# Side products dealt anew, two waits reordered and token copies split in a one-core diffusion step with DeltaNet heads and experts

## The chip, the cores and the metric

The kernel is one program on one core of a Trainium2 chip. The metric is the device time in microseconds of one execution. Smaller is better.

## What is computed

One step of a trunk with one layer, for 128 context tokens and 1024 latent tokens of width 1024. The parts the change touches are the DeltaNet mixer and the expert mixture:

```python
q = l2norm(q) * (DN_HEAD_DIM ** -0.5); k = l2norm(k)      # 8 heads of width 128
decay = exp(where(incl, g[..., :, None] - g[..., None, :], -inf))
lmat = where(strict, einsum('bhnck,bhnsk->bhncs', k_beta, k) * decay, 0.0)
a = lmat + eye                      # unit lower triangular, inverted per chunk
sol = triangular_solve(a, rhs)      # rhs from v and k
attn = einsum('bhnck,bhnsk->bhncs', q, k) * decay
# scan over the chunks, once forward and once backward:
v_new = u_c - w_c @ S;  o_c = q_c @ S + attn_c @ v_new;  S = S * d_c + k_c^T @ v_new
o = o_f + flip(o_b)
o = o * rsqrt(mean(o * o, -1) + EPS) * onorm_g * silu(gate)
...
# experts: each of 16 picks 128 latent and 16 context tokens
xs = h[idx]
ys = ((silu(xs @ w_gate) * (xs @ w_up)) @ w_down) * gates
```

## The kernel before

The instructions of each engine are written out by hand, and semaphores order them. PE is TensorE, DVE is VectorE, ACT is ScalarE, POOL is GpSimd, SP is SyncE with its DMA queue. "Head" is one pass of `body_pe`, `body_act`, `body_dve` and `body_pool`. Heads 0 to 6 are a loop on PE, ACT and DVE; head 7 is written out behind it.

**Side products.** A head needs little of TensorE at a time, with copies between its steps. So the input projection of the next head and of the merge gates is dealt into the gaps. A unit of it is eight matmuls into one bank (line 604), of 512 columns or, where its name ends in 0, of 128. `fill(place)` issues `FILLS[place]` of these matmuls, `evac(place)` on ACT copies out the units that end there (line 635), through `units_until`. A head has 18 units, the last head 21. `place` names run in the order of `PLACES`.

**A head on PE.** `fill("start")`; the sums of squares of k (`nk`) and q (`nq`), line 744; transposes of k and v (`kT`, `vT`, line 752); products k k and k q (line 762), the second of which waits until DVE has copied v out of its banks; transposes `LT` (line 771); two turns `Y2`; then six levels of an inverse by blocks. In a level, for two directions and three groups of three tiles: `Z` (line 788), a fill, `P` (line 788), a fill, and the turn `X` (line 779), which ACT copies out (line 935) before the next level's `Z` may write. ACT copies `Z` of direction 0, DVE that of direction 1 (line 1049); DVE takes `P` by a masked copy (line 1057). Behind the levels come `res`, `fix` and a scan over nine tiles with a fill of one matmul between its steps. `fill("end")` issues what is left of the side products, and then PE turns the normalised o (line 868).

**Norms and decays.** ACT squares q and k into `dm_flat[0]` and `dm_flat[1]`, and the inverse norms (`Ln`, `Exp`) come into the same places. DVE multiplies q and k by them (lines 1006 and 1007), and then writes the arguments of the decays of both directions over them: nine instructions each, line 1012. Then it copies v (line 1017). ACT takes `Exp` of the decays (line 916) and copies the products (line 921); POOL masks the decays; DVE multiplies them by k k (line 1023) for `LT`.

**End of a head.** POOL adds and squares o, DVE sums it (line 1109), ACT takes `Ln` and `Exp` (lines 975 and 977), DVE multiplies (line 1111), PE turns, DVE multiplies by the gate (lines 1118 to 1122) and marks the head's end. ACT's `evac("end")` stands ahead of its `Ln`. SP then stores the result with `store_b` (line 669), whose semaphore is `b_out`.

**Experts.** For expert e, PE makes the gate and up products in eight tiles (line 1968), turns the gathered tokens of expert e+1 (`turn_in`, lines 1942 and 1944) and makes eight down tiles (line 1982) with two banks in turn: tile 2 waits until ACT has copied tile 0 (lines 2014 and 2015). ACT's `evac_in`, 16 copies of the turned tokens (lines 1997 and 2001), stands ahead of the copy of tile 0:

```python
        if not last_e:
            evac_in(act, e + 1)
        for dt in range(KD):
            act.wait_ge(sem("dn_filled"), e * KD + dt + 1)
```

Of the kernel before, what the change touches and what calls it, by code (L numbers as in the profile page):

```python
# [19 lines left out]
P = 128  # L20
# [58 lines left out]
def build(nc, a, out_p, out_s, out_sf, out_sb, dbg=None, stop=99):  # L79
    ctx = ExitStack()  # L80
    with ctx:
        sems = {}

        def sem(name):
            if name not in sems:
                sems[name] = ctx.enter_context(nc.semaphore(name))
            return sems[name]
# [463 lines left out]
        ORDER_LAST = ("g1", "g0", "A0", "B0", "g2", "A1", "A2", "B1", "B2") + tuple(f"{x}{i}" for x in "CDEF" for i in range(3))  # L551

        FILLS = {"start": 3, "nk": 5, "nq": 12, "kk": 12, "LT": 16, "Y2f": 8, "Y2b": 8, "res": 2, "fix": 4}
        FILLS |= {f"Z{b}": 3 for b in LEVELS} | {f"P{b}": 3 for b in LEVELS}
        FILLS |= {f"scan{t}{x}": 1 for t in range(1, NT) for x in "abc"}
        PLACES = ["start", "nk", "nq", "kk", "LT", "Y2f", "Y2b"] + [f"{x}{b}" for b in LEVELS for x in "ZP"] + ["res", "fix"]
        PLACES += [f"scan{t}{x}" for t in range(1, NT) for x in "abc"] + ["end"]

        def units_until(order, place):

            if place == "end":
                return len(order)
            return sum(FILLS[p] for p in PLACES[:PLACES.index(place) + 1]) // KD

# [106 lines left out]
        def sync4(sp):  # L671
# [56 lines left out]
            sp.wait_ge(sem("b_out"), 16 * H)  # L728
            sp.dma_start(bT3[:, 0:H - 1, :], b_dram[0:(H - 1) * P, :].rearrange("(k p) t -> p k t", p=P)).then_inc(sem("b_in"), 16)

        def body_pe(pe, h, last_h=False):
            order = ORDER_LAST if last_h else ORDER
            side_work = projections(pe, h, order)

            def fill(place):
                for _ in range(FILLS.get(place, UNITS_MAX * KD)):
                    next(side_work, None)
# [3 lines left out]
            for d, name in ((1, "nk"), (0, "nq")):  # L741
                pe.wait_ge(sem("sq_ready"), 2 * h + 2 - d)
                for b, (at, n) in enumerate(SPAN):
                    nc.tensor.matmul(TRI[d][b][:, 0:n], ones, dm_flat[d][:, at:at + n], start=True, stop=True).then_inc(sem(f"filled{d}"), 1)  # L744
                fill(name)

            for d, name in ((0, "kT"), (1, "vT")):
# [49 lines left out]
            for lv, b in enumerate(LEVELS):  # L797
                for d in range(2):
                    products(d, f"Z{b}", [(nL[d], Ys[d])])
                fill(f"Z{b}")  # L800
                for d in range(2):
                    products(d, f"P{b}", [(Xs[d], Zs[d])])
                fill(f"P{b}")
                for d in range(2):
                    turn(d, f"X{b}", Ys)


            for d in range(2):
# [47 lines left out]
            for t in range(1, NT):  # L856
# [4 lines left out]
                fill(f"scan{t}b")  # L861
                advance(t)
                fill(f"scan{t}c")
            fill("end")
            pe.wait_ge(sem("o_normed"), h + 1)
            for g in range(3):
                for i in range(3):
# [6 lines left out]
        def body_act(act, h, last_h=False):  # L874
# [6 lines left out]
            def silu(j):  # L881
                act.wait_ge(sem("conv_done"), 3 * h + CONV_TURN.index(j))
                alone(act)
                for n, at in ((CTX, 0), (LAT, LAT0)):
                    last = nc.scalar.activation(qkvg[j][:, at:at + n], (k_next if j == 1 else qkvg[j])[:, at:at + n], ACT.Silu)
                if j == 2:
                    last.then_inc(sem("v_ready"), 1)
                else:
                    last.then_inc(sem("qk_silu"), 1)
                    act.wait_ge(sem("qk_silu"), 2 * h + 2 - j)  # L890
                    nc.scalar.activation(dm_flat[j][:, 0:CTX], qkvg[j][:, 0:CTX], ACT.Square)
                    nc.scalar.activation(dm_flat[j][:, CTX:T], qkvg[j][:, LAT0:LAT0 + LAT], ACT.Square).then_inc(sem("sq_ready"), 1)

            silu(1)
            silu(0)
# [6 lines left out]
            for d in (1, 0):  # L902
                for b, (at, n) in enumerate(SPAN):
                    filled(act, h, d, ("nq", "nk")[d], b)
                    nc.scalar.activation(dm_flat[d][:, at:at + n], TRI[d][b][:, 0:n], ACT.Ln, bias=eps_c).then_inc(sem(f"drained{d}_act"), 1)
                all_drained(act, h, d, ("nq", "nk")[d])
                nc.scalar.activation(dm_flat[d], dm_flat[d], ACT.Exp, scale=-0.5, bias=qscale_c if d == 0 else 0.0).then_inc(sem("rnorm"), 1)
                evac(("nq", "nk")[d])

            for g in range(3):  # L910
                filled(act, h, 0, "kT", g)
                nc.scalar.activation(flat(ktok, g), TRI[0][g][:, 0:384], ACT.Copy).then_inc(sem("drained0_act"), 1)

            for d in range(2):
                act.wait_ge(sem("gdiff"), 2 * h + d + 1)
                nc.scalar.activation(dm_flat[d], dm_flat[d], ACT.Exp).then_inc(sem("decay_exp"), 1)
            act.wait_ge(sem("b_out"), 16 * h + 16)
            for d in range(2):
                for g in range(3):
                    filled(act, h, d, ("kk", "kq")[d], g)  # L920
                    nc.scalar.activation(kq_flat[d][:, g * 384:(g + 1) * 384], TRI[d][g][:, 0:384], ACT.Copy).then_inc(sem(f"drained{d}_act"), 1)
# [19 lines left out]
            for b in LEVELS:  # L941
                copy(0, f"Z{b}", Zs)
                evac(f"Z{b}")
                evac(f"P{b}")
                for d in range(2):
                    copy(d, f"X{b}", Xs, F16)
            copy(0, "res", Zs)
            evac("res")
            evac("fix")
# [16 lines left out]
            for t in range(1, NT):  # L966
# [3 lines left out]
                evac(f"scan{t}b")  # L970
                outputs(t)
                evac(f"scan{t}c")
            evac("end")
            act.wait_ge(sem("o_sumsq"), h + 1)
            nc.scalar.activation(orow, orow, ACT.Ln, scale=1.0 / P, bias=eps_c).then_inc(sem("o_ln"), 1)
            act.wait_ge(sem("o_ln"), h + 1)
# [3 lines left out]
            for n, at in ((CTX, 0), (LAT, LAT0)):  # L980
                last = nc.scalar.activation(gateT[:, at:at + n], gateT[:, at:at + n], ACT.Silu)
            last.then_inc(sem("gate_ready"), 1)

        conv_to = (qT, k_next, vT)

# [15 lines left out]
            ins.then_inc(sem("tap_done" if tap < TAPS - 1 else "conv_done"), 1)  # L1001

        def body_dve(dve, h, last_h=False):
            for d, name in ((1, "k_normed"), (0, "q_normed")):
                dve.wait_ge(sem("rnorm"), 2 * h + 2 - d)
                nc.vector.tensor_tensor(qkvg[d][:, 0:CTX], qkvg[d][:, 0:CTX], dm_flat[d][:, 0:CTX], ALU.mult)
                nc.vector.tensor_tensor(qkvg[d][:, LAT0:LAT0 + LAT], qkvg[d][:, LAT0:LAT0 + LAT], dm_flat[d][:, CTX:T], ALU.mult).then_inc(sem(name), 1)
            for d in range(2):
                dve.wait_ge(sem(f"head_in{d}"), 32 * h + 32)
                dve.wait_ge(sem("q_normed" if d == 0 else "k_normed"), h + 1)  # L1010
                for t in range(NT):
                    last = nc.vector.tensor_scalar(dm_flat[d][:, t * P:(t + 1) * P], grow[d][:, t * P:(t + 1) * P],
                                                   tab["gc"][:, t, bass.ds(h + d * H, 1)], 0.0, ALU.subtract, ALU.min)
                last.then_inc(sem("gdiff"), 1)
            for g in range(3):
                filled(dve, h, 1, "vT", g)
                nc.vector.tensor_copy(flat(vtok, g), TRI[1][g][:, 0:384]).then_inc(sem("drained1_dve"), 1)

            for d in range(2):
                dve.wait_ge(sem("decay_masked"), 2 * h + d + 1)  # L1020
# [277 lines left out]
def later(nc, a, v, out_p, out_s, dbg, stop):  # L1298
# [691 lines left out]
        body9_pe(pe, E - 1, last_e=True)  # L1990
        turn_out(pe, E - 1)

    def evac_in(act, e):

        act.wait_ge(sem("xsT_filled"), e + 1)
        for k in range(KD):
            nc.scalar.activation(xsT[:, k, 0:CAP_L], banks[k // 4][:, (k % 4) * P:(k % 4 + 1) * P], ACT.Identity,  # L1997
                                 scale=amp2T[:, 1, k:k + 1], bias=modT3[:, 1, 3 * KD + k:3 * KD + k + 1])
        for k in range(KD):
            q, j = k // NJ, k % NJ  # L2000
            last = nc.scalar.activation(xsT[:, k, CAP_L:CAP], banks[2][:, j * QROWS + q * CAP_C:j * QROWS + (q + 1) * CAP_C], ACT.Identity,  # L2001
                                        scale=amp2T[:, 0, k:k + 1], bias=modT3[:, 0, 3 * KD + k:3 * KD + k + 1])
        last.then_inc(sem("xsT_ready"), 1)

    def body9_act(act, e, last_e=False):
        for f in range(KD):
            act.wait_ge(sem("gu_filled"), e * KD + f + 1)
            nc.scalar.activation(sil[f % 2], banks[3 + f % 2][:, 0:CAP], ACT.Silu).then_inc(sem("sil_ready"), 1)  # L2008
        if not last_e:
            evac_in(act, e + 1)  # L2010
        for dt in range(KD):
            act.wait_ge(sem("dn_filled"), e * KD + dt + 1)

            nc.scalar.activation(ysT[:, dt, 0:CAP_L], banks[5 + dt % 2][:, 0:CAP_L], ACT.Copy, scale=modT3[:, 1, 5 * KD + dt:5 * KD + dt + 1])  # L2014
            nc.scalar.activation(ysT_c[:, dt % NJ, dt // NJ * CAP_C:(dt // NJ + 1) * CAP_C], banks[5 + dt % 2][:, CAP_L:CAP], ACT.Copy, scale=modT3[:, 0, 5 * KD + dt:5 * KD + dt + 1]).then_inc(sem("dn_drained"), 1)  # L2015

    def act9(act):
        act.wait_ge(*at_step("gate2_ready"))
# [190 lines left out]
```

## Time and profile before

| what | value |
|---|---|
| median of 3 runs | 2760.51 us (2759.31 to 2762.32) |
| profiled execution, its own time | 2762.82 us |
| its span | 2760.9 us |
| PE busy | 2529.1 us, 92% of the span |
| DVE busy | 995.9 us, 36% |
| ACT busy | 929.7 us, 34% |
| POOL busy | 316.0 us, 11% |
| mean granted TensorE clock | 0.96 of full |

The span runs from the first to the last instruction; the profiled execution's own time is 1.9 us longer. The eight heads fill the time from about 145 to 1494 us, one each 167 us or so, and the experts that from about 1902 to 2725 us. PE is busy nearly all the time, so the places where it is idle are what to look at, and then whether what it waits for comes sooner.

### The profile page before, as it was taken

The page shows a single profiled execution, that of the slowest core. Times are in us where ns is not written, and L with a number is a line of the kernel's source. Part 1 is how long each engine was busy: PE and PEld are TensorE (multiplying, and loading weights), DVE is VectorE, ACT ScalarE, POOL GpSimd, SP SyncE. Part 2 cuts the span into 40 slices and gives each one's busy share as a digit, 9 for nine tenths or more (in the row PEclk, how much of TensorE's full clock was granted, in tenths as well). Part 3 has the DMA queues.
Part 4 walks back from the last instruction along what each step waited for, and adds up shares of the span by engine and source line. Part 5 has one row for each costly group of instructions (what it writes and reads, how often), then busy time and mean ns, then how long its engine had stood idle before and what let it go on. Part 6 is the DMA issues. An engine that isn't in the chain of part 4 may idle for free.

```text
span 2760.9 us, 42670 instructions
## 1 busy us (share of the span) xinstructions
PE 2529.1 (92%) x15886; PEld 1851.9 (67%) x15886; DVE 995.9 (36%) x2059; ACT 929.7 (34%) x2354; POOL 316.0 (11%) x212
## 2 busy tenths in 40 slices
PE   6789899998999989899999999964999999999994
PEld 3356565665656656566565555434999999999994
DVE  2445454554536545464442442373001010010012
ACT  3144543535445354443542111331221321322322
POOL 0012120211202112121110000000101101101100
PEclk8989999999999999999999999986999999999997
DMA  8511102011020211101124232226777877878864
GB/s 304 202 39 33 61 24 71 1 33 61 24 71 1 58 36 33 61 1 53 35 99 151 105 119 72 104 93 231 271 259 259 288 251 266 288 243 269 293 235 154
DMA packets 196575, 362.67 MB, mean 131 GB/s; under 512 B 8922, under 2 KB 70311, under 8 KB 193355
## 3 DMA queue, kind: packets, MB, share of 16 engines
q1 hardware_dynamic: 190027, 341.77, 35.7%
q0 software_dynamic: 6400, 18.88, 2.8%
q8 instruction: 99, 1.62, 0.2%
q14 instruction: 49, 0.40, 0.0%
HBM read 319.97 MB, written 40.65 MB: 131 GB/s over the span
## 4 chain that ended last, share of the span: by engine, by line
PE 86%; DVE 5%; ACT 5%; issue 2%; DMA 1%; SPq 0%; DVEq 0%; POOL 0%; ACTq 0%; POOLq 0%
PE bank L604 29%; PE bank L1968 18%; PE bank L1982 7%; PE bank L788 6%; PE bank L1403 5%; PE bank L1648 4%; PE bank L1421 2%; PE bank L779 2%; ACT arena L1997 2%; PE bank L844 1%; PE bank L833 1%; ACT arena L2001 1%; PE bank L850 1%; PE bank L744 1%; PE bank L825 1%
## 5 line engine op out<-in xcount | busy, mean ns | idle before, releaser
L604 PE MATMUL bank<-arena 128*128 128x512 f32 (+1 forms) x2496 | 893.6, 498 | 41.3 <-issue 23.4
L604 PEld LDWEIGHTS bank<-arena 128*128 128x128 f32 x2496 | 395.7, 194 | 309.2 <-issue 307.1
L1968 PE MATMUL bank<-arena 128*128 128x144 f32 x4096 | 512.8, 286 | 5.1 <-ACT arena L2001 5.1
L1968 PEld LDWEIGHTS bank<-arena 128*128 128x128 f32 x4096 | 509.5, 190 | 5.3 <-ACT arena L2001 5.3
L2048 DVE TENSOR_TENSOR arena<-arena,bank 128x144 f32<-128x144 f32 x128 | 38.9, 304 | 730.1 <-ACT arena L2008 730.1
L1982 PE MATMUL bank<-arena 128*128 128x144 f32 x2048 | 261.3, 287 | 20.2 <-ACT arena L2015 19.5
L1982 PEld LDWEIGHTS bank<-arena 128*128 128x128 f32 x2048 | 254.6, 189 | 24.7 <-ACT arena L2015 22.7
L935 ACT ACTIVATE arena<-bank 128x384 f16<-128x384 f16 (+1 forms) x504 | 200.8, 525 | 165.8 <-PE bank L779 165.8
L635 ACT ACTIVATE arena<-bank 128x512 f32<-128x512 f32 (+1 forms) x156 | 76.3, 489 | 401.3 <-PE bank L604 401.0
L2008 ACT ACTIVATE arena<-bank 128x144 f32<-128x144 f32 x128 | 37.2, 290 | 464.4 <-PE bank L1968 464.4
L788 PE MATMUL bank<-arena 128*128 128x128 f16 x2304 | 183.5, 220 | 6.7
L788 PEld LDWEIGHTS bank<-arena 128*128 128x128 f16 x2304 | 139.1, 98 | 71.3 <-ACT arena L935 36.6
L1057 DVE CAST_PREDICATED arena<-arena,bank 128x384 f16<-128x384 uint32 x288 | 138.9, 553 | 98.6 <-PE bank L788 98.5
L1049 DVE CAST arena<-bank 128x384 f16<-128x384 f32 x168 | 83.8, 552 | 158.8 <-PE bank L788 158.8
L1000 DVE SCALAR_TENSOR_TENSOR arena<-arena 128x1156 f32<-128x1156 f32 x96 | 136.0, 1417 | 0.4
L1648 PE MATMUL bank<-arena 128*128 128x512 f32 x288 | 129.9, 604 | 1.7 <-DVE arena L1558 1.7
L1403 PE MATMUL bank<-arena 128*128 128x384 f32 x384 | 127.1, 493 | 1.8 <-DVE arena L1123 1.8
L1403 PEld LDWEIGHTS bank<-arena 128*128 128x128 f32 x384 | 73.7, 192 | 55.0 <-issue 3.8
L2014 ACT ACTIVATE arena<-bank,arena 128x128 f32<-128x128 f32 x128 | 49.2, 390 | 149.8 <-PE bank L1982 149.8
L1648 PEld LDWEIGHTS bank<-arena 128*128 128x128 f32 x288 | 54.0, 193 | 65.6 <-issue 65.5
L955 ACT ACTIVATE arena<-bank,arena 128x128 f32<-128x128 f32 x144 | 53.3, 370 | 109.8 <-PE bank L833 109.4
L779 PEld LDWEIGHTS bank<-arena 128*128 128x128 f16 x1008 | 61.6, 98 | 33.2 <-issue 31.5
(258 smaller groups left out, 2573.2 us busy)
## 6 DMA issues: line engine op xcount, KB each, us to landing
arena<-in_exp_w_gate SPq DMA_DIRECT2D x32, 2048.0 KB, 10.7
arena<-in_exp_w_up SPq DMA_DIRECT2D x32, 2048.0 KB, 15.9
arena<-in_exp_w_down SPq DMA_DIRECT2D x32, 2048.0 KB, 9.1
arena<-in_w_in SPq DMA_DIRECT2D x52, 512.0 KB, 5.1
arena<-in_ada_w SPq DMA_DIRECT2D x24, 1024.0 KB, 7.4
side_dram<-arena SPq DMA_DIRECT2D x20, 576.0 KB, 3.2
arena<-side_dram SPq DMA_DIRECT2D x20, 576.0 KB, 3.9
arena<-g_dram SPq DMA_DIRECT2D x16, 576.0 KB, 4.8
```

Source lines behind the costliest of these rows:

```text
L604: ins = nc.tensor.matmul(unit_bank(order, name)[:, 0:n], w[:, k, :], hT3[:, k, at:at + n], start=(k == 0), stop=(k == KD - 1))
L635: nc.scalar.activation(dst, bank[:, 0:n], ACT.Copy).then_inc(sem("pj_drained"), 1)
L779: last = nc.tensor.transpose(TRI[d][g].bitcast(F16)[:, i * P:(i + 1) * P], src[d][:, 3 * g + i, :], ident_h)
L788: last = nc.tensor.matmul(TRI[d][g][:, i * P:(i + 1) * P], lhs if lhs.shape[1] == P else lhs[:, 3 * g + i, :], rhs if rhs.shape[1] == P el ...
L935: nc.scalar.activation(flat(dst[d], g), src[:, 0:384], ACT.Copy).then_inc(sem(f"drained{d}_act"), 1)
L1000: ins = nc.vector.scalar_tensor_tensor(conv_to[j][:, 0:CW], raw[j][:, tap:tap + CW], w, conv_to[j][:, 0:CW], ALU.mult, ALU.add)
L1049: nc.vector.tensor_copy(flat(Zs[1], g), TRI[1][g][:, 0:384]).then_inc(sem("drained1_dve"), 1)
L1057: nc.vector.copy_predicated(Ys[d][:, 3 * g:3 * g + 3, :], masks[:, 1 - d, lv + 1, :].unsqueeze(1).to_broadcast([P, 3, P]), TRI[d][g][:, 0: ...
L1403: last = nc.tensor.matmul(banks[n % RING][:, 0:CH], w_dn[half][:, k, col:col + P], bT3[:, k, c * CH:(c + 1) * CH], start=(k == 0), stop=(k ...
L1648: last = nc.tensor.matmul(banks[2 * (i % 2) + half][:, 0:512], mixT3[:, k, t * P:(t + 1) * P], w_outs[:, k, half * 512:(half + 1) * 512], ...
L1968: last = nc.tensor.matmul(banks[3 + f % 2][:, m * CAP:(m + 1) * CAP], w_unit[2 * half + m][:, k, col:col + P], xsT[:, k, :], start=(k == 0 ...
L1982: last = nc.tensor.matmul(banks[5 + dt % 2][:, 0:CAP], w_unit[4 + half][:, k, col:col + P], hid[:, k, :], start=(k == 0), stop=(k == KD - 1))
```

## The change

In the heads:

- The three side products behind `Z` become two, and one goes to a new place behind the turn `X`. The six of a level stay six; ACT has an `evac` at the new place.
- `"end"` becomes `"end1"` (six matmuls) and `"end2"` (the rest). PE issues both where it issued `"end"`. ACT copies the units of `"end1"`, then does the norm of o and the gate's Silu, and then copies those of `"end2"`.
- The norms of q and k swap their buffers (`norms`). So the decay arguments of direction 0 can be written as soon as k is normalised, ahead of q's norm; those of direction 1 come behind the copies of v.
- ACT does `Exp` of direction d and then the copies of the product of d, where it did both `Exp` first. The wait for `b_out` goes ahead of both.

In the experts, `evac_in` goes in pieces of two k's (four copies) behind the copies of down tiles 0, 1, 2 and 3.

```diff
-        FILLS |= {f"Z{b}": 3 for b in LEVELS} | {f"P{b}": 3 for b in LEVELS}
+        FILLS |= {f"Z{b}": 2 for b in LEVELS} | {f"P{b}": 3 for b in LEVELS} | {f"X{b}": 1 for b in LEVELS} | {"end1": 6}
...
+        norms = (dm_flat[1], dm_flat[0])
...
                 for d in range(2):
                     turn(d, f"X{b}", Ys)
+                fill(f"X{b}")
...
-            fill("end")
+            fill("end1")
+            fill("end2")
             pe.wait_ge(sem("o_normed"), h + 1)
...
+            act.wait_ge(sem("b_out"), 16 * h + 16)
             for d in range(2):
                 act.wait_ge(sem("gdiff"), 2 * h + d + 1)
                 nc.scalar.activation(dm_flat[d], dm_flat[d], ACT.Exp).then_inc(sem("decay_exp"), 1)
-            act.wait_ge(sem("b_out"), 16 * h + 16)
-            for d in range(2):
                 for g in range(3):
                     filled(act, h, d, ("kk", "kq")[d], g)
...
                 for d in range(2):
                     copy(d, f"X{b}", Xs, F16)
+                evac(f"X{b}")
...
-            evac("end")
+            evac("end1")
             act.wait_ge(sem("o_sumsq"), h + 1)
...
             last.then_inc(sem("gate_ready"), 1)
+            evac("end2")
...
+            normalise(1, "k_normed")
+            decay_arguments(0)
+            normalise(0, "q_normed")
             for g in range(3):
                 filled(dve, h, 1, "vT", g)
                 nc.vector.tensor_copy(flat(vtok, g), TRI[1][g][:, 0:384]).then_inc(sem("drained1_dve"), 1)
+            decay_arguments(1)
...
-        if not last_e:
-            evac_in(act, e + 1)
+
         for dt in range(KD):
             act.wait_ge(sem("dn_filled"), e * KD + dt + 1)
...
+            if not last_e and dt < KD // 2:
+                evac_in(act, e + 1, range(2 * dt, 2 * dt + 2))
```

## Rows read from the trace of the kernel before

**Rows 1.** The page: its first line.

```profile
span 2760.9 us, 42670 instructions
```

**Rows 2.** Waits of PE, whole span: who waited <- for whom, total us, times, longest.

```profile
PE bank L604 <- issue: 23.4, 6, 5.0
PE bank L868 <- DVE arena L1111: 20.1, 8, 2.5
PE bank L1982 <- ACT arena L2015: 19.5, 15, 1.3
...
PE bank L762 <- DVE arena L1017: 17.1, 8, 2.2
```

**Rows 3.** Timeline of a level of head 2: start us, us, engine, line [idle before].

```profile
530.60 1.17 PE L779 MATMUL bank<-arena 128*128 128x128 f16 x18
...
530.97 3.56 ACT L935 ACTIVATE arena<-bank 128x384 f16<-128x384 f16 x9 [6.09 <-PE bank L779]
...
531.60 2.17 PE L788 MATMUL bank<-arena 128*128 128x128 f16 x18
...
533.61 2.79 PE L604 MATMUL bank<-arena 128*128 128x512 f32 x6
...
536.24 1.21 PE L788 MATMUL bank<-arena 128*128 128x128 f16 x18
...
537.29 2.79 PE L604 MATMUL bank<-arena 128*128 128x512 f32 x6
```

**Rows 4.** Timeline of norms, decays and products of head 2.

```profile
496.62 1.22 DVE L1007 TENSOR_TENSOR arena<-arena 128x1024 f32<-128x1024 f32 x1
...
497.99 4.64 DVE L1012 TENSOR_SCALAR arena<-arena 128x128 f32<-128x128 f32 x18
...
502.54 1.47 DVE L1017 COPY arena<-bank 128x384 f32<-128x384 f32 x3
...
503.14 2.27 PE L762 MATMUL bank<-arena 128*128 128x128 f32 x18 [2.13 <-DVE arena L1017]
...
505.00 2.95 DVE L1023 TENSOR_TENSOR arena<-arena 128x384 f32<-128x384 f32 x6 [0.98 <-ACT arena L921]
...
507.94 2.13 PE L771 MATMUL bank<-arena 128*128 128x128 f32 x18
```

**Rows 5.** Timeline of the end of head 1 and the return to head 2.

```profile
460.08 13.04 PE L604 MATMUL bank<-arena 128*128 128x512 f32 x30
...
466.77 1.35 DVE L1109 TENSOR_REDUCE arena<-arena 128x9 f32<-128x1152 f32 x1 [4.70 <-POOL arena L1167]
...
473.16 0.60 ACT L635 ACTIVATE arena<-bank 128x512 f32<-128x512 f32 x1 [6.27 <-PE bank L604]
...
475.63 2.18 PE L868 MATMUL bank<-arena 128*128 128x128 f32 x9 [2.51 <-DVE arena L1111]
...
476.77 1.28 ACT L885 ACT_TABLE_LOAD   x1
...
478.87 0.35 SPq L669 DMA_DIRECT2D b_dram<-arena  x1
...
479.57 1.04 ACT L892 ACTIVATE arena<-arena 128x1024 f32<-128x1024 f32 x1
...
481.21 4.98 PE L604 MATMUL bank<-arena 128*128 128x512 f32 x6 [3.40 <-issue]
```

**Rows 6.** Windows: stretch, us, busy us of PE, PEld, DVE, ACT, POOL, granted clock, DMA share, GB/s.

```profile
481.20:486.20 5.00, 4.99 (x8) 2.21 (x9) 0.00 (x0) 4.24 (x6) 0.00 (x0) 0.57 0.02 5
```

**Rows 7.** Timeline where the loop of heads is left, head 6 to 7.

```profile
1312.75 3.85 PE L604 MATMUL bank<-arena 128*128 128x512 f32 x6
```

**Rows 8.** Timeline of one expert, down tiles.

```profile
2039.53 2.90 ACT L1997 ACTIVATE arena<-bank,arena 128x128 f32<-128x128 f32 x8 [0.85 <-PE bank L1944]
...
2042.28 2.19 ACT L2001 ACTIVATE arena<-bank,arena 128x16 f32<-128x16 f32 x8
...
2044.94 12.12 PE L1982 MATMUL bank<-arena 128*128 128x144 f32 x96 [1.30 <-ACT arena L2015]
...
2047.22 0.37 ACT L2014 ACTIVATE arena<-bank,arena 128x128 f32<-128x128 f32 x1 [1.91 <-PE bank L1982]
```

More of the change, by code:

```diff
@@ L553, in build @@
         FILLS = {"start": 3, "nk": 5, "nq": 12, "kk": 12, "LT": 16, "Y2f": 8, "Y2b": 8, "res": 2, "fix": 4}
-        FILLS |= {f"Z{b}": 3 for b in LEVELS} | {f"P{b}": 3 for b in LEVELS}
+        FILLS |= {f"Z{b}": 2 for b in LEVELS} | {f"P{b}": 3 for b in LEVELS} | {f"X{b}": 1 for b in LEVELS} | {"end1": 6}
         FILLS |= {f"scan{t}{x}": 1 for t in range(1, NT) for x in "abc"}
-        PLACES = ["start", "nk", "nq", "kk", "LT", "Y2f", "Y2b"] + [f"{x}{b}" for b in LEVELS for x in "ZP"] + ["res", "fix"]
-        PLACES += [f"scan{t}{x}" for t in range(1, NT) for x in "abc"] + ["end"]
+        PLACES = ["start", "nk", "nq", "kk", "LT", "Y2f", "Y2b"] + [f"{x}{b}" for b in LEVELS for x in "ZPX"] + ["res", "fix"]
+        PLACES += [f"scan{t}{x}" for t in range(1, NT) for x in "abc"] + ["end1", "end2"]
         def units_until(order, place):
-            if place == "end":
+            if place == "end2":
                 return len(order)
@@ L743, in body_pe @@
                 for b, (at, n) in enumerate(SPAN):
-                    nc.tensor.matmul(TRI[d][b][:, 0:n], ones, dm_flat[d][:, at:at + n], start=True, stop=True).then_inc(sem(f"filled{d}"), 1)
+                    nc.tensor.matmul(TRI[d][b][:, 0:n], ones, norms[d][:, at:at + n], start=True, stop=True).then_inc(sem(f"filled{d}"), 1)
                 fill(name)
@@ L890, in silu @@
                     act.wait_ge(sem("qk_silu"), 2 * h + 2 - j)
-                    nc.scalar.activation(dm_flat[j][:, 0:CTX], qkvg[j][:, 0:CTX], ACT.Square)
-                    nc.scalar.activation(dm_flat[j][:, CTX:T], qkvg[j][:, LAT0:LAT0 + LAT], ACT.Square).then_inc(sem("sq_ready"), 1)
+                    nc.scalar.activation(norms[j][:, 0:CTX], qkvg[j][:, 0:CTX], ACT.Square)
+                    nc.scalar.activation(norms[j][:, CTX:T], qkvg[j][:, LAT0:LAT0 + LAT], ACT.Square).then_inc(sem("sq_ready"), 1)
             silu(1)
@@ L904, in body_act @@
                     filled(act, h, d, ("nq", "nk")[d], b)
-                    nc.scalar.activation(dm_flat[d][:, at:at + n], TRI[d][b][:, 0:n], ACT.Ln, bias=eps_c).then_inc(sem(f"drained{d}_act"), 1)
+                    nc.scalar.activation(norms[d][:, at:at + n], TRI[d][b][:, 0:n], ACT.Ln, bias=eps_c).then_inc(sem(f"drained{d}_act"), 1)
                 all_drained(act, h, d, ("nq", "nk")[d])
-                nc.scalar.activation(dm_flat[d], dm_flat[d], ACT.Exp, scale=-0.5, bias=qscale_c if d == 0 else 0.0).then_inc(sem("rnorm"), 1)
+                nc.scalar.activation(norms[d], norms[d], ACT.Exp, scale=-0.5, bias=qscale_c if d == 0 else 0.0).then_inc(sem("rnorm"), 1)
                 evac(("nq", "nk")[d])
@@ L1003, in body_dve, with normalise, decay_arguments @@
         def body_dve(dve, h, last_h=False):
[L1004 to L1008, printed above, removed]
+            def normalise(j, name):
+                dve.wait_ge(sem("rnorm"), 2 * h + 2 - j)
+                nc.vector.tensor_tensor(qkvg[j][:, 0:CTX], qkvg[j][:, 0:CTX], norms[j][:, 0:CTX], ALU.mult)
+                nc.vector.tensor_tensor(qkvg[j][:, LAT0:LAT0 + LAT], qkvg[j][:, LAT0:LAT0 + LAT], norms[j][:, CTX:T], ALU.mult).then_inc(sem(name), 1)
+            def decay_arguments(d):
                 dve.wait_ge(sem(f"head_in{d}"), 32 * h + 32)
-                dve.wait_ge(sem("q_normed" if d == 0 else "k_normed"), h + 1)
+                dve.wait_ge(sem("k_normed" if d == 0 else "q_normed"), h + 1)
                 for t in range(NT):
@@ L1991, in pe9, with evac_in @@
         turn_out(pe, E - 1)
-    def evac_in(act, e):
-        act.wait_ge(sem("xsT_filled"), e + 1)
-        for k in range(KD):
+    def evac_in(act, e, ks=range(KD)):
+        if ks[0] == 0:
+            act.wait_ge(sem("xsT_filled"), e + 1)
+        for k in ks:
             nc.scalar.activation(xsT[:, k, 0:CAP_L], banks[k // 4][:, (k % 4) * P:(k % 4 + 1) * P], ACT.Identity,
                                  scale=amp2T[:, 1, k:k + 1], bias=modT3[:, 1, 3 * KD + k:3 * KD + k + 1])
-        for k in range(KD):
             q, j = k // NJ, k % NJ
@@ L2002, in evac_in @@
                                         scale=amp2T[:, 0, k:k + 1], bias=modT3[:, 0, 3 * KD + k:3 * KD + k + 1])
-        last.then_inc(sem("xsT_ready"), 1)
+        if ks[-1] == KD - 1:
+            last.then_inc(sem("xsT_ready"), 1)
     def body9_act(act, e, last_e=False):
```

## The prediction

> **What bounds the kernel now.** I read the page first: the span is 2760.9 us [rows 1], and PE is busy 92% of it, so time can only come from places where PE is idle or slow. The second view is PE's waits over the whole span [rows 2]. Three of its rows name the very partners that the change moves. The turn of o (L868) waits for the norm at the end of each of the 8 heads, 20.1 us in all; the k q product (L762) waits in each head for DVE's copy of v, 17.1 us; the third down tile (L1982) waits in 15 experts for ACT's copy of the first, 19.5 us. The fourth row, 23.4 us of "issue" in 6 returns of the loop, is touched by no edit. The third view is the timeline, for two things: what stands behind each wait, and waits too short for that table. Such a one is in the levels: nine groups of copies run on ACT while PE makes Z in small steps [rows 3].
>
> **Part 1, the side product behind the turn X.** The X turns begin at 530.60 and ACT copies six groups of them at 3.56/9 = 0.40 us each, 530.97 to about 533.34. Z may write a group only when it is copied, so Z starts at 531.60 and takes until the fill at 533.61: 2.01 us. P, the same 18 matmuls with nothing to wait for, takes 537.29 - 536.24 = 1.05 us [rows 3]. PE loses 0.96 us per level. A side product of 512 columns costs a third of the fill of three, (536.24 - 533.61)/3 = 0.88 us. Put between X and Z it ends at about 532.1; three of the six groups are copied by then, the others set Z's end at 533.6 as before. So the product costs nothing there, and the fill behind Z is 0.88 us shorter. What that fill hid: the copies of Z. ACT ends the last at 530.97 + 3.56 = 534.53; P would start at 536.24 - 0.88 = 535.36, so 0.8 us of cover is left. If a unit's copy (0.60 us, as L635 in [rows 5]) falls between the X and Z copies, 0.2 us is left. The fill behind P keeps three. Six levels have five X-to-Z passages; behind the sixth turn comes `res`, with three terms per tile, 9 matmuls a group against 3, slower than the copies, and there I count nothing. So 5 x 0.88 = 4.4 us per head; in the last head two of the units in the levels have 128 columns, and I count three: 7 x 4.4 + 2.6 = 33.4 us. Bounds: 0 if the copies turn out to set the period, 8 x 5 x 0.96 = 38 us if the whole loss goes.
>
> **Part 2, decays.** DVE has q normalised at 497.84, then makes 18 decay arguments in 4.64 us, and only then copies v (1.47 us) [rows 4]. Nine of them, 2.32 us, move ahead of q's norm, into a time in which DVE waits for ACT, and nine behind the copies of v. The v copies then run from about 498 to 499.6, the k q product needs no wait, and the 2.13 us idle [rows 4] goes. What comes late next is the chain behind the second set of arguments (Exp, mask, multiply): it ended at 502.6 and ends at about 501.9 now, 0.7 us earlier, while PE comes 2.1 us earlier to LT. In the trace the multiplications ran 505.00 to 507.95 and LT 507.94 to about 510 [rows 4]: LT takes its last group some 1.7 us behind the multiplication. The chain loses 1.4 us against PE, so it just fits. I take the full row, 17.1 us; if nothing were hidden it would be 8 x 0.7 = 5.6 us, the low bound. The high bound is 17.1. ACT's Exp of direction 0 is no longer late, and its copies of k k move little. The wait for `b_out` now blocks ACT some microseconds sooner, at about 498.7; the store is issued at 478.87 [rows 5], 20 us before, so it costs nothing.
>
> **Part 3, norm of o.** The sum of squares is ready at 466.77 + 1.35 = 468.12, but ACT's Ln stands behind the last copy at 473.16 [rows 5]. Behind `end1` alone, it starts at 468.2; Ln, Exp and DVE's multiplication take about 2 us (from the copy's end at 473.76 to 475.63, less hops), so o is normalised at about 470.2, and PE finds it ready when its fills end at 473.13: 2.51 us go, at each of 8 ends, 20.1 us [rows 2, 5]. PE doesn't wait for the later copy of the last unit, since that still starts at 473.16; the gate's Silu is over by about 471.3. In the last head five units end behind this point instead of two. The norm is over before the second of them is full, so its copy isn't late.
> The clock: in the row at 481.20 to 486.20 the granted clock is 0.57, and three side products take 4.98 us where [rows 3] has 2.63 [rows 5, 6]. PE had been idle 2.51 us and then 3.40 us. Where the loop is left there is no return, and the three still take 3.65 us to the next group (3.85 as merged in [rows 7]) behind the one idle stretch of 2.5 us. Without that stretch I expect the full clock there: 1.0 us, and 0.6 us for the turns ahead of it. The same at the way out of head 7: 3 us together. At the six returns the 3.4 to 5.0 us of "issue" stay, the clock falls for them alone, and I count nothing; bounds 0 and 6 x 2.35 = 14 us.
> Against it: ACT now returns right behind a copy that ends at 473.76, where before it had 2.6 us of gate Silu between. PE's return costs 3.4 to 5.0 us of idle time [rows 2], ACT's showed none: its table load stands at 476.77 directly behind its last work. If ACT's return costs as much as PE's, it goes on at 477.2 to 478.8. PE asks for k's squares at about 481.21 - 2.5 + 5.0 = 483.7, and they are ready 480.61 - 476.77 = 3.84 us after the return [rows 5], at 482.6 at the latest. So 1 us is left and I take 0; if ACT's return took 6.5 us, it would cost about 0.4 us per return. The Trainium skill, Runtime: NRT & Kernel Launch, section on instruction fetch mechanics, says that a taken branch to a page outside the two held makes the sequencer wait for a DMA fetch; the gaps of 3.4 to 5.0 us on PE agree with it, and by it a gap on ACT is to be expected, which no row of this trace shows. It changes the sum only past that 1 us.
>
> **Part 4, experts.** Before tile 0 is copied ACT does 2.90 + 2.04 = 4.94 us of token copies, and PE idles 1.30 us [rows 8]. Cut in four they are 1.24 us a tile; with a tile's own two copies (0.53 us to the end of both, 0.37 the first) ACT needs about 1.8 us per tile, PE 12.12/6 = 2.02 us. Tile 0 is copied 0.6 us after it is full, two tiles before its bank is needed. All 15 waits go: 19.5 us. The tokens are ready at about 2049, behind tile 3, and the next expert begins at about 2057. If mixed shapes cost ACT 0.3 us more per tile it would pass PE's pace, and one tile in two would wait a few tenths: bound 15 us.
>
> **Sum.** 33.4 + 17.1 + 20.1 + 3.0 + 19.5 = 93.1 us. Some copies of units that now stand ahead of X copies move behind them, a few tenths per head, so I take 96. The profiled execution's own time, 2762.8, goes to 2667; it is 2.3 us above the median of the runs shown, so I forecast **2665 us**.
>
> **Rivals.**
> (a) The levels give nothing: the ring from X copies to Z copies to masked P copies has a partner other than PE, and the shorter fill behind Z shows up as a wait at P. For it: ACT's nine copies are contiguous, and cover falls from 1.7 to 0.8 us. Against it: 0.8 us is left. 2665 + 33 = 2698 us.
> (b) The second decay chain is what LT waits for, or ACT's return is exposed: 2665 + 12 = 2677 us; with both, 2690 us.
> (c) More than forecast: the clock stays up at the returns. 2665 - 14 = 2651 us.
> (d) Slower. The store of b lands so late that ACT, now waiting for it ahead of the Exp of the decays, holds up mask, LT and all behind it. The price is one microsecond per microsecond per head behind the 20 us of slack; it decides from a landing more than 32 us behind the issue, since 8 x 12 us are won otherwise. Nothing in the trace points to such a transfer. At 35 us it gives 2665 + 8 x 15 = 2785 us.
> (e) The reordering does nothing because each wait only changes its partner: PE then waits at the same places for something else, 2760 us. It needs all four parts to fail.
>
> **How the numbers follow.** Forecast within 10 us 0.55; (a) fully or half 0.10; (b) 0.15; (c) or other small gains 0.15; (d) 0.02; (e) 0.03. The range reaches from (c) to (b) with both: 2649 to 2688 us, which holds 0.83 or so. A change within 0.2% (5.5 us) is about what a measurement of this kernel cannot tell from none. Faster by more 0.95, within 0.02, slower 0.03.
>
> **What would show it.** In PE's waits the rows of L762 and L1982 are gone or below 3 us, and that of L868 too; "issue" at L604 stays between 20 and 30 us. A level (from one X turn to the next) takes 8.45 us instead of 9.33, with Z's end following X's start by 3.0 us as before. The turn of o follows the last side product directly. The clock is full at the way out of the loop. It would be wrong if PE waits at P for L935 or L1049, if LT waits for L1023, if L744 waits for ACT's squares, or if down tiles wait for L2015 still.

## The result and the profile after

The changed kernel takes 2619.1 us (median of 4 runs, 2618.2 to 2620.4) against 2761.05 us (2759.3 to 2762.3) beside it: a ratio of 0.9484, 95% interval 0.9470 to 0.9498. That is 142 us less where 96 us were forecast, and 30 us below the lower end of the range. The profiled execution's span went from 2760.9 to 2616.6 us.

The waits of PE over the whole span (who waited, for whom, total us, times, longest), to be set beside [rows 2]; "issue" is idle time in which the profile shows nothing that PE waits for:

```profile
PE bank L1871 <- DVE arena L1856: 23.5, 1, 23.5
PE bank L604 <- DMA arena<-in_w_in: 16.3, 1, 16.3
...
PE bank L747 <- ACT arena L897: 4.2, 6, 1.0
...
PE bank L604 <- issue: 0.5, 2, 0.3
```

All four rows of [rows 2] are gone, also the one that I had left standing: "issue" at L604 fell from 23.4 to 0.5 us. One small wait is new: PE asks for k's squares (L747, which was L744) up to 1.0 us before ACT has them.

A level of head 2 in the timeline, beside [rows 3]:

```profile
493.67 1.17 PE L782 MATMUL bank<-arena 128*128 128x128 f16 x18
...
494.04 3.56 ACT L939 ACTIVATE arena<-bank 128x384 f16<-128x384 f16 x9 [5.24 <-PE bank L782]
494.68 1.08 PE L604 MATMUL bank<-arena 128*128 128x512 f32 x2
...
495.59 1.25 PE L791 MATMUL bank<-arena 128*128 128x128 f16 x18
...
496.68 1.93 PE L604 MATMUL bank<-arena 128*128 128x512 f32 x4
...
498.45 1.21 PE L791 MATMUL bank<-arena 128*128 128x128 f16 x18
...
502.13 1.17 PE L782 MATMUL bank<-arena 128*128 128x128 f16 x18
```

From the X turn to the fill behind Z it is 496.68 - 493.67 = 3.01 us, as before (533.61 - 530.60), but now with a side product inside; the level takes 502.13 - 493.67 = 8.46 us.

The products of head 2 in the timeline, beside [rows 4]: one block of 36 matmuls without a gap, LT begins 6.7 us behind its start.

```profile
464.71 1.49 DVE L1028 COPY arena<-bank 128x384 f32<-128x384 f32 x3
...
465.17 4.18 PE L765 MATMUL bank<-arena 128*128 128x128 f32 x36
...
466.12 2.83 DVE L1019 TENSOR_SCALAR arena<-arena 128x128 f32<-128x128 f32 x9
...
471.55 1.50 DVE L1035 TENSOR_TENSOR arena<-arena 128x384 f32<-128x384 f32 x3 [1.20 <-POOL arena L1151]
471.87 2.13 PE L774 MATMUL bank<-arena 128*128 128x128 f32 x18
```

The end of head 1 and the return, beside [rows 5]:

```profile
442.74 0.30 ACT L980 ACTIVATE arena<-arena 128x9 f32<-128x9 f32 x1 [1.27 <-DVE arena L1121]
...
443.31 1.36 DVE L1123 TENSOR_TENSOR arena<-arena 128x1152 f32<-128x1152 f32 x1 [0.61 <-ACT arena L982]
...
447.54 1.15 PE L873 MATMUL bank<-arena 128*128 128x128 f32 x9
...
447.73 0.60 ACT L635 ACTIVATE arena<-bank 128x512 f32<-128x512 f32 x1 [1.88 <-PE bank L604]
...
448.35 1.28 ACT L890 ACT_TABLE_LOAD   x1
...
448.78 2.84 PE L604 MATMUL bank<-arena 128*128 128x512 f32 x6
...
452.24 2.21 PE L747 MATMUL bank<-arena 128*128 128x128 f32 x6 [0.62 <-ACT arena L897]
```

The norm of o is ready at 444.67, three microseconds before PE wants it. PE turns o in 1.15 us instead of 2.18 and goes on at once, and the three side products behind it take 2.84 us, not 4.98. ACT, too, returns without a gap: its copy ends at 448.33, the table load begins at 448.35.

The down tiles of an expert, beside [rows 8]: eight tiles in one block, the token copies in pieces between.

```profile
1865.54 16.07 PE L1994 MATMUL bank<-arena 128*128 128x144 f32 x128
...
1867.82 0.37 ACT L2026 ACTIVATE arena<-bank,arena 128x128 f32<-128x128 f32 x1 [3.02 <-PE bank L1994]
...
1869.18 0.39 ACT L2013 ACTIVATE arena<-bank,arena 128x16 f32<-128x16 f32 x1
1869.80 0.37 ACT L2026 ACTIVATE arena<-bank,arena 128x128 f32<-128x128 f32 x1 [0.23 <-PE bank L1994]
```

ACT needs 1867.82 to 1869.57 = 1.75 us per tile and then waits 0.23 us for the next.

Where the 144.3 us of the two spans are, from the starts of these groups in all heads of both traces:

| stretch | before, us | after, us | less in all | forecast |
|---|---|---|---|---|
| first Z to the scan | 7 x 64.62, 55.26 | 7 x 60.06, 51.89 | 35.3 | 33.4 |
| turn of k (`kT`) to LT | 12.71, 6 x 11.06, 11.10 | 8 x 8.67 | 20.8 | 17.1 |
| end of the scan's last matmul to the turn of o | 7 x 15.39, 30.91 | 7 x 12.71, 28.23 | 21.4 | 20.1 |
| turn of o to the next sum of squares of k, six returns | 10.40 to 10.89 | 4.71 | 35.7 | 0 |
| the same where the loop is left, and out of head 7 | | | 4.8 | 3.0 |
| experts | 821.8 | 797.95 | 23.9 | 19.5 |
| the rest | | | 2.4 | |

### The profile page after: what moved, and what is told of

Read it like the earlier page. It is cut to its first block, busy times and chain, and to the rows that moved or that the text cites. A ratio compares the mean times of both kernels' runs of the same rounds, so it can differ in the third digit from the quotient of the medians.

```text
span 2616.6 us, 42677 instructions
## 1 busy us (share of the span) xinstructions
PE 2468.1 (94%) x15886; PEld 1834.8 (70%) x15886; DVE 995.4 (38%) x2059; ACT 932.4 (36%) x2354; POOL 316.0 (12%) x212
## 4 chain that ended last, share of the span: by engine, by line
PE 92%; DVE 3%; ACT 2%; DMA 1%; issue 1%; SPq 0%; POOL 0%; DVEq 0%; ACTq 0%; POOLq 0%
PE bank L604 31%; PE bank L1980 19%; PE bank L1994 10%; PE bank L791 5%; PE bank L1415 5%; PE bank L1660 5%; PE bank L1433 2%; PE bank L782 2%; PE bank L848 1%; PE bank L837 1%; PE bank L747 1%; PE bank L854 1%; PE bank L765 1%; PE bank L829 1%; PE bank L852 1%; DMA arena<-in_ada_w 1%
## 5 line engine op out<-in xcount | busy, mean ns | idle before, releaser
L604 PE MATMUL bank<-arena 128*128 128x512 f32 (+1 forms) x2496 | 890.0, 493 | 18.5 <-DMA arena<-in_w_in 16.3
L604 PEld LDWEIGHTS bank<-arena 128*128 128x128 f32 x2496 | 386.8, 192 | 254.8 <-issue 252.7
L791 PE MATMUL bank<-arena 128*128 128x128 f16 x2304 | 153.0, 219 | 0.0
```

Of the source, the lines that this page charges most:

```text
L604: ins = nc.tensor.matmul(unit_bank(order, name)[:, 0:n], w[:, k, :], hT3[:, k, at:at + n], start=(k == 0), stop=(k == KD - 1))
L791: last = nc.tensor.matmul(TRI[d][g][:, i * P:(i + 1) * P], lhs if lhs.shape[1] == P else lhs[:, 3 * g + i, :], rhs if rhs.shape[1] == P el ...
```

## The experiments

Each was timed beside the kernel before (2761.08, 2760.93 and 2760.72 us in the three sets). Stretches of time are taken from the profiled execution of each kernel. The first question was the 35.7 us at the returns, the second whether the four parts add up.

### The norm of o alone

Kernel before with `end1`, `end2` and their copies as in the change, nothing else.

> Only the norm of o goes between the last copies, everything else as before. In the changed kernel the idle time of 3.4 to 5.0 us at the loop's return is gone, which the prediction had left standing. Theory A (PE's sequencer runs ahead of the array; before the change the wait for the normed o held it back until the last fill had run out, so the branch and its fetch of instructions began late and lay open; without that wait they lie under queued matmuls): the 20 us of the wait, the 23 us of the return and 10 to 15 us of half clock all go with this part alone, 2700 us, and issue at L604 is below 2 us. Theory B (the return got shorter because other parts moved the transfers that collide with the fetch): this part alone gives the 20 us of the wait and little of the return, 2738 us, and issue stays above 15 us.

Measured: 2713.9 us, ratio 0.9825 (0.9808 to 0.9841), 47.2 us less. From the turn of o to the next squares of k all six returns take 4.70 or 4.71 us, as with the whole change, and of the "issue" this is left:

```profile
PE bank L604 <- issue: 0.8, 3, 0.3
```

So the return belongs to this part and theory B falls. But the time is 14 us above A's 2700. The same stretches as in the table above show where it is: from `kT` to LT six heads now take 12.98 or 12.99 us and the last 12.84 where before it was 11.06 and 11.10. The timeline of head 1, products, and windows over it (columns as in [rows 6]; the granted clock stands behind the five busy times):

```profile
323.47 2.17 PE L762 MATMUL bank<-arena 128*128 128x128 f32 x18
328.07 3.90 PE L762 MATMUL bank<-arena 128*128 128x128 f32 x18 [2.42 <-DVE arena L1019]
```

```profile
327.00:328.00 1.00, 0.00 (x0) 0.00 (x0) 1.00 (x3) 0.41 (x1) 0.47 (x1) 1.00 0.00 0
328.00:329.00 1.00, 0.93 (x5) 0.93 (x6) 0.94 (x3) 1.00 (x2) 0.08 (x1) 0.67 0.00 0
329.00:330.00 1.00, 1.00 (x7) 1.00 (x6) 0.07 (x1) 1.00 (x4) 1.00 (x1) 0.50 0.00 0
```

The idle time of 2.4 us at L762 is an old one (2.13 us in [rows 4]). Here the clock fell to half (1.2 of 2.4 GHz) around it in all eight heads, where in the kernel before it did so in head 0 alone. The k q product took 3.90 us in place of 2.27.

### Levels alone

Kernel before with 2, 3, 1 and the new place `X`.

> Only the side products dealt 2, 3, 1. By the ledger of the two traces (64.62 to 60.06 us from the first Z to the scan in seven heads, 55.26 to 51.89 in the last) 35 us go: 2726 us. The return stays as before, issue near 23 us. If the parts help each other, less: the prediction's own sum was 33 us, 2728 us.

Measured: 2732.8 us, ratio 0.9894 (0.9878 to 0.9911), 28.3 us less. First Z to the scan takes 60.06 us in seven heads and 51.89 in the last, to 0.01 us the values of the whole change: 35.3 us. "Issue" is 23.7 us. The difference is the same clock: `kT` to LT takes 12.60 to 12.69 us in four of heads 1 to 7, 1.6 us more than before, which makes 6.3 of the missing 7.

### Decays alone

> Only the decays and the norms' buffers. By the traces' ledger 17 to 21 us go (2.39 us per head from kT to LT, 4.04 in head 0): 2742 us. If the late second chain shows without the other parts, 6 us: 2755 us.

The edit is the buffers of the norms, the two sets of decay arguments and ACT's order, as in the change. Measured: 2737.1 us, ratio 0.9909 (0.9893 to 0.9926), 24.0 us less. `kT` to LT takes 8.66 us in every head. 20.8 us are there; the rest is where the loop is left, 3.70 us where it was 5.30, and small things at the returns.

### Experts alone

> Only the token copies between down tiles. The wait as the rows gave it was 19.5 us; the ledger says 23.9 us, 1.6 us for each of 15 experts, since the idle time of a row leaves out the restart of the weight pipeline behind it: 2737 us against 2741 us by the row.

Measured: 2737.6 us, ratio 0.9913 (0.9896 to 0.9929), 23.5 us less, as the ledger has it and 4 us more than the row of the wait.

### A wait of 0.7 us put in

The changed kernel with one wait more on PE, for the copy of the head's last unit:

```diff
             fill("end2")
+            pe.wait_ge(sem("pj_drained"), unit_at(h, order[-1]))
             pe.wait_ge(sem("o_normed"), h + 1)
```

> The changed kernel, but PE waits for ACT's copy of the last unit before it turns o. The copy ends 0.6 us after the last fill, so as a wait it costs 8 x 0.65 = 5 us. Theory A (a wait at the loop's end holds PE's sequencer, and the fetch of the return lies open behind it): issue of 3 to 5 us comes back at each of six returns and with it the half clock in most of them, 25 to 35 us more: 2645 to 2655 us. Theory B (collision of transfers, or the length of idle time before): 5 us more, 2624 us, issue below 2 us.

Measured: 2657.05 us (2652.9 to 2657.5), ratio 0.9619 (0.9603 to 0.9635): 38 us more than the changed kernel. The timeline of the end of head 1:

```profile
455.12 1.20 PE L874 MATMUL bank<-arena 128*128 128x128 f32 x9 [0.69 <-ACT arena L635]
...
459.62 2.92 PE L604 MATMUL bank<-arena 128*128 128x512 f32 x3 [3.30 <-issue]
```

The wait itself is 0.69 us, and the stretch from the scan to the turn grows by 0.86 us a head, 6.8 us. The six returns grow from 4.71 to 9.03 to 9.65 us each, 28.4 us. So a wait that holds PE up directly ahead of the branch makes the return dear, and it did so for both things that PE was made to wait for, the normed o before and a copy here. The granted clock is 0.50 again in the side products behind the gap (459.60 to 462.00).

### PE's loop written out

```diff
-                with pe.Fori(0, H - 1) as h:
+                for h in range(H - 1):
                     body_pe(pe, h)
```

First on the kernel before, then on the kernel with the wait put in.

> The kernel before with PE's loop over heads 0 to 6 written out; the other engines keep their loops. Theory A, with the taken branch as its cause: the wait for the normed o stays, 20 us, the issue of 23.4 us goes, and a part of the half clock (it also followed the idle 2.5 us where the loop is left), 2760 - 23 - 3 to 8 = 2730 to 2735 us. If the idle time at the return is not the branch's, 2760 us.

> The changed kernel with the wait for the last copy, and PE's loop written out. Theory A: wait and return only cost together; what is left is the wait itself, 5 us and at most some half clock, 2624 us. If the wait costs by itself more than its length, 2645 us or more as with the loop.

Measured: 2737.25 us for the first, ratio 0.9916 (0.9899 to 0.9932), with no "issue" row at L604 left and the wait for the norm as it was, 20.1 us. The returns take 5.13 to 5.29 us instead of 10.40 to 10.89, 33 us less; 8.5 us of it are given back from `kT` to LT, where five heads take 12.92 to 13.00 us at half clock. Measured for the second: 2621.9 us, ratio 0.9495 (0.9479 to 0.9510), 35 us less than with the loop and within 3 us of the changed kernel. So the wait without a taken branch behind it costs no more than its own length: the stretch from the scan to the turn grows by 6.8 us as with the loop, and the six stretches behind the turn take 3.95 us instead of 4.71, 4.6 us less, since the wait at L747 is gone. With the branch it costs 35 us more. The Trainium skill says of a taken branch (Runtime: NRT & Kernel Launch, instruction fetch mechanics) that, where its target isn't held, it "forces a DMA fetch of the target page before execution can continue". The gaps of 3.0 to 5.0 us in the kernel before and in this one agree with that.

### Work put between the wait and the branch

The kernel with the wait put in, and behind the turn of o in heads 0 to 6 four products of 512 columns into a free bank, which nobody reads:

```diff
+            if not last_h:
+                for _ in range(4):
+                    nc.tensor.matmul(TRI[1][1][:, 0:512], ident, hT3[:, 0, CTX:CTX + 512], start=True, stop=True)
```

> The kernel with the wait for the last copy (2657 us), and in heads 0 to 6 four products of 512 columns more behind the turn of o, whose result nobody reads: 3.4 us of added work a head, 24 us in seven. Theory A (PE's sequencer runs ahead of the array, so work queued between the wait and the branch hides the fetch): the idle 3.0 to 3.5 us at the return is filled by this work, the clock stays up, and the six returns take about as long as before or up to 2 us less; only head 6 pays its 3.4 us: 2645 to 2660 us. If the fetch begins only when the queue has run out, the work adds to the gap: 2681 us and issue near 19 us as before it.

Measured: 2645.6 us, ratio 0.9583 (0.9567 to 0.9599): 11.5 us faster than without this work, though 3.44 us of it are added seven times. The chain of work at the end of head 1 (start, us, what):

```profile
450.47 0.61 ACT arena L635
451.07 0.04 issue
451.12 1.20 PE bank L874 x9
452.32 3.44 PE bank L878 x8
455.75 2.58 PE bank L604 x6
```

The added work takes the place of the gap, and the clock stays full: the three side products take 2.58 us. It only just suffices: in two of the six returns there is 0.35 us more. Six returns go from 9.03 to 9.65 us each to 7.05 to 7.43, 13.6 us less in all, and head 6, which has no return, pays 3.4 us.

### Other deals of the side products

The changed kernel with 1, 3, 2 and with 3, 2, 1 behind Z, P and X.

> The changed kernel with the side products dealt 1 behind Z, 3 behind P and 2 behind X. The first behind X already covers the stall but for about 0.1 us, so a second can gain nothing more, and one behind Z (0.88 us) is about what the copies of Z need by themselves. If the prediction's 0.8 us of cover was right, no loss or a few tenths a level: 2619 to 2630 us. If the copies of Z set the pace sooner, 0.5 us and more a level: above 2643 us.

> The changed kernel with three behind Z, two behind P, one behind X. The masked copies end 3.4 us after P begins, P itself takes 1.05 us and two products 1.75 us, so X starts group by group as DVE lets it; X's copies on ACT, which set Z's end, start a little later. At most 0.6 us a level lost, 48 levels: 2619 + 10 to 29 = 2629 to 2648 us. If only the sum of products in a level mattered, 2619 us.

Measured: 2617.8 us (2615.7 to 2618.3) and 2621.0 us (2618.6 to 2622.2), ratios 0.9482 (0.9466 to 0.9498) and 0.9492 (0.9477 to 0.9508). First Z to the scan is 59.83 and 60.06 us, against 60.06 with 2, 3, 1. So the prediction's 0.8 us of cover behind Z was there. My expectation for 3, 2, 1 was wrong: a loss of 10 us and more, and there is none clear of the noise. I had let X wait for the last masked copy. It waits group by group, and a timeline of that run shows X beginning at 493.39, 2.8 us behind P, in the middle of the masked copies, with PE 10.00 of 10 us busy:

```profile
490.57 1.21 PE L791 MATMUL bank<-arena 128*128 128x128 f16 x18
...
491.05 2.88 DVE L1069 CAST_PREDICATED arena<-arena,bank 128x384 f16<-128x384 uint32 x6 [1.78 <-PE bank L791]
491.62 1.93 PE L604 MATMUL bank<-arena 128*128 128x512 f32 x4
...
493.39 1.17 PE L782 MATMUL bank<-arena 128*128 128x128 f16 x18
```

What counts in a level, among these deals, is that at least one product stands behind X.

### Norm and decays together

> The norm of o and the decays, without the other two parts. Alone they gave 47 and 24 us, 71 together: 2690 us if they add up. In the run with the norm alone the stage from the turn of k to LT took 12.99 us where before it took 11.06, with the clock at half behind the idle time at L762; without that idle time it cannot, 8.66 us. So with both 47 + 24 + 7 x 1.9 = 84 us should go: 2677 us.

Measured: 2680.4 us, ratio 0.9709 (0.9692 to 0.9725), 80.3 us less; the two alone gave 71.2. `kT` to LT takes 8.66 us in every head, so with the idle time gone the clock no longer falls there. That the parts help each other is confirmed, the size (84) was 4 us too high: the decays alone also shorten the way out of the loop (by 1.6 us) and the returns (by 1.2 us), which the norm's part does as well, and that can be won only once.

### Four side products at the start

```diff
-        FILLS = {"start": 3, "nk": 5, ...
+        FILLS = {"start": 4, "nk": 4, ...
```

> The changed kernel with four side products at start and four behind the sum of squares of k, where it has three and five. In its trace PE waits 0.4 to 1.0 us at L747 for ACT's squares of k in six heads, 4.2 us. One more product (0.86 us) at the start covers that, and k's normalisation was ready 1.9 us before it was asked for, so the shorter fill behind it costs nothing: 2614 us. If ACT's chain is what bounds the head's start, no change, 2619 us.

Measured: 2613.4 us (2611.9 to 2615.4), ratio 0.9468 (0.9452 to 0.9484), against 2619.1 (2618.2 to 2620.4) for the changed kernel in another set. The wait at L747 is gone from the list, and from the sum of squares of k to `kT` it is 10.1 us instead of 10.96 in five heads. It is the fastest kernel of this study. The two intervals of the ratio overlap, the runs' own ranges don't.

## Why the prediction was wrong

**The direction and all four mechanisms held.** What I named as their signs is in the trace: the rows of L762, L868 and L1982 gone, a level of 8.46 us (8.45 forecast) with Z's end as before, the turn of o directly behind the last fill, the clock full where the loop is left. Two signs came out the other way: "issue" at L604 is 0.5 us and not 20 to 30, and L747 does wait for ACT's squares, 4.2 us. Rival (a) is excluded by the level's timeline, (b)'s first half by LT starting in the middle of DVE's multiplications (471.87 against 471.55 for the second three) without a wait.

**The step that failed** is in part 3: "At the six returns the 3.4 to 5.0 us of "issue" stay, the clock falls for them alone, and I count nothing; bounds 0 and 6 x 2.35 = 14 us." They went, 35.7 us with all that hung on them, three quarters of the 46 us missed. Even rival (c) had only the clock at the returns in it, not the gap. I took the gap as a price of the return. It was the price of a return behind a wait that held PE up.

The reading that fits: before, PE's sequencer stood at the wait for the normed o until 475.6, behind it had only the turn to issue, and met the branch when the array had nothing queued. Without the wait it runs ahead of the array, past the turn and the branch, while side products are still queued. The packets of the DMA queue "instruction" bear this out. The pages of the kernel before and of the same kernel with PE's loop written out have these lines:

```profile
q8 instruction: 99, 1.62, 0.2%
```

```profile
q8 instruction: 84, 1.38, 0.2%
```

Only PE's program differs between the two, and the other queue of that name, q14, has 49 packets in both. So q8 is PE's. At the end of head 1 its packet is in 478.40:478.50 before and in 445.50:446.00 after the change (`--dma` over these windows: packets, MB, share of 16 engines):

```profile
q8 instruction: 1, 0.02, 70.5%
```

```profile
q8 instruction: 1, 0.02, 16.3%
```

Before, that is 5.3 us behind the last fill, which ended at 473.13, and after it is at least 1.7 us ahead of the last fill's end (447.71). With the wait of 0.7 us put in, the packet is in 456.20:456.30, behind the turn's start at 455.12. With PE's loop written out in the kernel before there is none from 462 to 477, around the turn at 468.77. That the wait ahead of the branch is the cause is shown by four runs: with another wait put there the gap comes back (38 us), with the loop written out that wait costs 3 us, with the norm alone the gap goes, and work queued behind the wait hides it. How little queued work would do is open, since only four products were tried; so is why the packet comes 2.8 to 3.4 us behind the turn's start in the kernel before and 1.1 to 1.4 us behind it with the wait put in.

I could have come to it. I had set the Trainium skill's rule on taken branches beside PE's gap, but asked what a later branch would cost on ACT alone, and not when PE's sequencer comes to its own. ACT's return shows no gap in any of these traces (0.02 us ahead of the table load each time), so (b)'s second half did not come true; ACT's squares are late only because PE itself now comes earlier than I thought.

**Terms mis-sized.** The experts: 23.9 us against 19.5. From the first down tile to the next gate tile it was 17.48 us (2039.42 to 2056.90) and is 15.91 (1865.54 to 1881.45), 1.57 us less and not the 1.30 of the wait's row. The rest is the start behind a wait: the copy of the first tile comes 2.28 us behind its start (2044.94 to 2047.22, and in the changed kernel 1865.54 to 1867.82), those of the next tiles 1.98 us apart, so each wait costs 0.3 us more than its row shows. The decays: 20.8 us against 17.1, 1.65 us of it the half clock behind the idle time in head 0, the rest 0.26 us a head, which I take to be of the same kind as with the experts. I had called 17.1 the high bound. My 2.32 us for nine arguments, half of 4.64, wasn't right for either nine: they take 1.86 us ahead of q's norm and 2.83 us behind the copies of v. The levels: 35.3 against 33.4, 4.56 us a head for 4.4 and 3.4 for 2.6 in the last. The way out of head 7: I had 1.6 us beyond the wait, it was 3.1. The 2.9 us that I added for copies of units to come from 93.1 to 96 have no row of their own in the table. Of the 2.4 us of its last row 1.2 lie ahead of head 0, where no edit is.

**The parts don't add up.** Alone they give 47.2, 28.3, 24.0 and 23.5 us, 123.0 in all; together 142. The missing 19 us are the clock in the main: the old idle time at L762 drops it in more heads with one part made than in the kernel before, in seven more with the norm alone, in four with the levels, in one with the experts, at 1.6 to 1.9 us each, 21 us in all. Against that the way out of the loop, 1.6 us, is counted both with the norm and with the decays.

## What to carry to other kernels

At the end of a hardware loop look not only at how long an engine waits but at what it has queued behind the wait: a wait of 0.7 us directly ahead of the branch cost 5.6 us per pass here, and four products of no use between the two gave 2 us of it back. Have the last wait ahead of the branch satisfied before the engine comes to it, or put work between the two. Short idle stretches are worth closing together, since what one costs in clock depends on where the others have moved it.

## What the hardware showed that I had not expected

- PE's return in the loop of heads: 3.0 to 5.1 us of idle time when a wait just ahead of it holds PE up, 0 to 0.3 us when nothing does or when four products stand between.
- Nearly the same idle time at L762, 2.1 to 2.2 us in the kernel before and 2.2 to 2.4 us with the norm alone, left the granted clock full in seven of eight heads of the first, and went with half the clock in all eight of the second. The same edit can so be worth 2.39 or 4.3 us per head. What decides it no run shows.
- Of DVE's arguments of the decays one takes 1.2 to 1.3 us in each head, before the change as after it; the others take 0.28 us. In head 2 it is the one that starts within 0.03 us of a POOL mask: 501.32 beside 501.29 before, 466.31 beside 466.29 after. Nine with it among them take 2.83 us, nine without 1.86 us.
